# An up projection of seven block-sum products in place of eight block products, in a two-layer hybrid decoder step

## The reference

```python
def conv_ffn(xn, buf, w_up, w_conv, b_conv, w_down):
    u, gt = jnp.split(xn @ w_up, 2, axis=-1)
    t = u.shape[1]
    up = jnp.concatenate([buf.astype(u.dtype), u], axis=1)
    conv = b_conv
    for j in range(CONV_W):
        conv = conv + w_conv[j] * up[:, j:j + t]
    y = (jax.nn.silu(conv) * gt) @ w_down
    return y, up[:, -(CONV_W - 1):]
```

## Time and profile before

| what | value |
|---|---|
| median of three runs | 1718.83 us |
| span of the profiled execution (the page gives no other time for it) | 1719.7 us |
| TensorE matmul / weight load busy | 1637.4 us (95%) / 1481.8 us (86%) |
| VectorE, ScalarE, GpSimd busy | 926.0, 617.1, 181.0 us |
| TensorE instructions | 14807 |
| matmuls of the up projection, L1399 | 4032, 30% of the chain that ended last |
| matmuls of the down projection, L1472 | 2088, 15% of that chain |
| DMA | 219 MB, mean 128 GB/s |

### The profile page before, as it was taken

How to read it: one execution, slowest core, us unless ns; L and a number is a source line. 1 busy time by engine, 2 the same in 40 slices (tenths; PEclk the granted TensorE clock), 3 DMA queues, 4 the chain that set the end, 5 groups by cost and what they waited for, 6 DMA issues and landing times.

```text
span 1719.7 us, 37383 instructions
## 1 busy us (share of the span) xinstructions
PE 1637.4 (95%) x14807; PEld 1481.8 (86%) x14807; DVE 926.0 (54%) x2434; ACT 617.1 (36%) x1215; POOL 181.0 (11%) x290
## 2 busy tenths in 40 slices
PE   6999999988999999999989999998799999999998
PEld 5899875558999999999989997655689999999997
DVE  3544446656564555645564354575656464555644
ACT  3322246534451322413342213664334232423314
POOL 1011104511100000000001101242210000000001
PEclk9999999999999999999989999999999999999999
DMA  9436297468521321221133536634944122322201
GB/s 345 128 97 186 95 362 222 120 207 145 196 88 61 99 99 62 101 84 50 53 100 92 182 114 236 220 89 150 167 114 165 52 98 99 99 79 69 99 25 58
DMA packets 156544, 219.43 MB, mean 128 GB/s; under 512 B 11466, under 2 KB 116362, under 8 KB 155932
## 3 DMA queue, kind: packets, MB, share of 16 engines
q1 hardware_dynamic: 151488, 201.45, 37.5%
q0 software_dynamic: 4896, 15.71, 3.6%
HBM read 208.77 MB, written 16.68 MB: 131 GB/s over the span
## 4 chain that ended last, share of the span: by engine, by line
PE 87%; DVE 4%; DMA 3%; ACT 2%; SPq 1%; issue 1%; DVEq 1%; POOL 1%; ACTq 0%
PE ps L1399 30%; PE ps L1472 15%; PE ps L921 13%; PE ps L1351 5%; PE ps L764 3%; PE ps L1060 2%; PE ps L1045 2%; PE ps L972 2%; DMA slab<-in_w_out 2%; PE ps L905 1%; PE ps L1383 1%; PE ps L916 1%; PE ps L915 1%; PE ps L1017 1%; DMA big<-in_cache_win_kv 1%
## 5 line engine op out<-in xcount | busy, mean ns | idle before, releaser
L1399 PE MATMUL ps<-work_r,big_r 128*128 128x272 f32 x1344 | 279.2, 289 | 2.2 <-ACT work L1910 1.1
L1399 PE MATMUL ps<-work_r,slab_r 128*128 128x272 f32 x1344 | 278.5, 288 | 0.0
L1399 PE MATMUL ps<-xnT_r,big_r 128*128 128x272 f32 x1344 | 276.4, 287 | 0.0
L1399 PEld LDWEIGHTS ps<-work_r,big_r 128*128 128x128 f32 x1344 | 210.1, 188 | 4.7 <-issue 4.7
L1399 PEld LDWEIGHTS ps<-xnT_r,big_r 128*128 128x128 f32 x1344 | 211.7, 188 | 0.0
L1399 PEld LDWEIGHTS ps<-work_r,slab_r 128*128 128x128 f32 x1344 | 210.6, 188 | 0.0
L921 PE MATMUL ps<-slab_r,work_r 128*128 128x256 f32 x960 | 205.6, 282 | 0.0
L2078 DVE TENSOR_TENSOR slab_r<-slab,big_r 128x2048 fp32r<-128x2048 f32 (+1 forms) x84 | 170.7, 2035 | 52.2 <-ACT big_r L1874 42.1
L1913 ACT ACTIVATE big<-big,work 128x560 f32<-128x560 f32 x44 | 33.6, 765 | 371.4 <-DVE big L2736 371.4
L921 PEld LDWEIGHTS ps<-slab_r,work_r 128*128 128x128 f32 x960 | 157.8, 188 | 2.7 <-issue 2.5
L1472 PE MATMUL ps<-side_r,big_r 128*128 128x272 f32 x696 | 145.7, 291 | 0.8 <-DVE big_r L2078 0.8
(11 more groups left out here) (498 smaller groups left out, 3172.2 us busy)
## 6 DMA issues: line engine op xcount, KB each, us to landing
slab<-in_w_mod SPq DMA_DIRECT2D x22, 2048.0 KB, 10.5
slab<-in_w_up SPq DMA_DIRECT2D x44, 1024.0 KB, 7.7
slab<-in_w_in SPq DMA_DIRECT2D x20, 1024.0 KB, 6.4
slab<-in_w_down SPq DMA_DIRECT2D x20, 1024.0 KB, 6.8
slab<-in_cache_cmp_kv SPq DMA_DIRECT2D x128, 128.0 KB, 2.0
slab<-in_cache_sel_kv SPq DMA_DIRECT2D x96, 128.0 KB, 2.1
big<-in_cache_win_kv SPq DMA_DIRECT2D x16, 512.0 KB, 7.5
out<-in_cache_win_kv POOLq DMA_DIRECT2D x16, 508.0 KB
```

What stands on the lines that cost most here:

```text
L1399: ins = mm(ps[2 * half + b][:, 0:HALF], wt, fr(x[:, k, HALF * b:HALF * b + HALF]), start=k == 0 and n == 0, stop=k == KC - 1 and n == 2)
```

## The change

Chunks 0 to 3 stay as they were. For chunks 4 to 21 (CL = 4) the two by two by two block structure of [u; gate] = weights x inputs (weights U_K1, U_K2, G_K1, G_K2 of 512 columns, inputs K1/K2 x t1/t2) is computed with seven products of sums of blocks, M1 to M7, in place of eight products of blocks. Each product is 4 k x 3 = 12 matmuls of 272 columns.

- Per layer, `input_sums` on GpSimd makes four sums of input blocks (T1 to T4, 1088 columns each, eight operations); ScalarE and VectorE split them.
- Per chunk, `block_sum` on GpSimd makes four weight sums of 512 columns. Seven weight operands are split per chunk, in a ring of four slots: the high parts by ScalarE, the low parts of M1, M5, M6, M3, M7 by VectorE, those of M2 and M4 by GpSimd.
- Product results are added in PSUM where two follow each other in one bank (M1 + M6 + M7 + M4 in one, M5 + M3 in another), and ScalarE copies the intermediate sums out (M1, M5, M1 + M6, 272 columns each). VectorE adds the copies back for u's two halves and the gate's second half. The first tap, the tail and the history copies go to ScalarE.
- The loop over chunks is unrolled on all engines. Up weights come one chunk at a time (1 MB, rows of 512 B) into a pair of buffers in slab 2; `split_down` goes in quarters of 1024 columns. Several semaphores are merged.

TensorE's order, and the product:

```diff
-                four_chunks(0, first=True)
-                for j in range(1, NG):
-                    four_chunks(j)
...
+                m1(CL)
+                m2(CL)
+                down(4, 0)
+                m5(CL)
+                m6(CL)
+                m3(CL)
+                m7(CL)
+                for c in range(CL + 1, FC):
+                    m1(c)
+                    m4(c - 1)
+                    m5(c)
+                    m2(c)
+                    m6(c)
+                    if c % 4 == 0:
+                        down(4, c // 4 - 1)
+                    m3(c)
+                    m7(c)
                 down(2, NG, last=True)
...
+                def product(kind, c, bank, new):
+                    n = nth(kind, c)
+                    pe.wait_ge(*low_at(kind, c, L))
+                    xh, xl = FACTOR[kind]
+                    for k in range(4):
+                        wh, wl = [fr(r[n % RING][:, 128 * k:128 * k + 128]) for r in (ring_hi, ring_lo)]
+                        for m, (wt, x) in enumerate(((wh, xh), (wh, xl), (wl, xh))):
+                            ins = mm(ps[bank][:, 0:HALF], wt, fr(x[:, k, :]), start=new and k == 0 and m == 0, stop=k == 3 and m == 2,
+                                     skip_group_check=True)
+                    ins.then_inc(b_acc.sem, 1)
+                def m4(c):
+                    pe.wait_ge(c_g2.sem, c_g2.at(nc_(c), L))
+                    product("M4", c, PBANK[c % 2], False)
```

ScalarE's order:

```diff
+                for c in range(CL + 1, FC):
+                    g, q = c // 4, c % 4
+                    product1_out(c)
+                    high("M6", c)
+                    silu(1, c - 1)
+                    history_in(c)
+                    high("M3", c)
+                    if g < NG and q in (1, 2):
+                        split_down(2 * q - 2, 1)
+                    product5_out(c)
+                    high("M7", c)
+                    split_h((c - 1) % 4, c - 1)
+                    if c + 1 < FC:
+                        high("M1", c + 1)
+                    if g < NG and q in (1, 2):
+                        split_down(2 * q - 1, 1)
+                    sum6_out(c)
+                    high("M4", c)
+                    if c + 1 < FC:
+                        high("M5", c + 1)
...
+                    first_tap(c)
+                    if c + 1 < FC:
+                        high("M2", c + 1)
+                    tail_kept(c)
```

VectorE's order:

```diff
+                for c in range(CL + 1, FC):
+                    g, q = c // 4, c % 4
+                    low_block("M6", c)
+                    hidden_block(c - 1)
+                    low_block("M3", c)
+                    if g < NG and q in (1, 2):
+                        split_down(2 * q - 2, 1, g)
+                    low_block("M7", c)
+                    split_h((c - 1) % 4, c - 1)
+                    u_first(c)
+                    if c + 1 < FC:
+                        low_block("M1", c + 1)
+                    if g < NG and q in (1, 2):
+                        split_down(2 * q - 1, 1, g)
+                    if q == 0:
+                        for m in range(8):
+                            add_y(g - 1, m)
+                    u_second(c)
+                    if c + 1 < FC:
+                        low_block("M5", c + 1)
+                    else:
+                        for part in range(2):
+                            split_down(part, 1, NG)
+                    gate_second(c)
+                    other_taps(c)
```

GpSimd's order, and SP's loads of the up weights:

```diff
+                input_sums()
+                low_block("M2", CL)
...
+                for c in range(CL + 1, FC):
+                    block_sum("M5", c)
+                    low_block("M4", c - 1)
+                    block_sum("M6", c)
+                    low_block("M2", c)
+                    block_sum("M3", c)
+                    block_sum("M7", c)
+                low_block("M4", FC - 1)
...
+                def load_raw(c):
+                    if c < CL + 2:
+                        sp.wait_ge(g_acc.sem, g_acc.at(2, L))
+                        sp.wait_ge(w_hi.sem, w_hi.at(3, L))
+                    else:
+                        sp.wait_ge(*low_at("M4", c - 2, L))
+                    dst = raw_up[c % 2].rearrange("p (h k n) -> p h k n", h=2, k=8)
+                    for h in range(2):
+                        sp.dma_start(dst[:, h, :, :], wup[L, :, :, h, 128 * c:128 * c + 128]).then_inc(raw_loads(c, L)[0], 16)
```

More of the change, by code:

```diff
@@ new lines, in sum_at, with low_at, nc_ @@
+        def sum_at(kind, c, L):
+            return b_sum.sem, b_sum.at(4 + 4 * (c - CL) + ("M5", "M6", "M3", "M7").index(kind) + 1, L)
+        def low_at(kind, c, L):
+            on_pool = kind in LOW_POOL
+            before = [(m, f) for f in range(CL, FC) for m in ROUND if (m in LOW_POOL) == on_pool and nth(m, f) < nth(kind, c)]
+            return b_lo[on_pool].sem, b_lo[on_pool].at(len(before) + 1 + (4 if before and not on_pool else 0), L)
+        def nc_(c):
+            return c - CL + 1
@@ new lines, in _ @@
+                for q in range(CL):
+                    u_chunk(q % 2, q)
+                    if q < 2:
+                        if q == 0:
+                            act.wait_ge(slab_in[0], slab_loads("ffn", 0, L))
+                        split_w(q + 2, q + 2)
+                    if q == 2:
+                        high("M1", CL)
+                    if q == 3:
+                        high("M2", CL)
+                        history_in(CL)
+                    split_h(q, q)
+                    if q == 1:
+                        act.wait_ge(slab_in[1], slab_loads("ffn", 1, L))
+                    for k in ((), (0, 1), (2, 3), ())[q]:
+                        split_down(k, 1)
@@ L2727, in conv @@
                     n = UPW - 2
[L2728 removed]
+                    ts_(cv[:, s, 0:n], up[:, s, 0:n], column(cd), None, ALU.mult)
                     drain()
[L2730 to L2732 removed]
@@ L2768, in _, with add_y @@
[L2768 to L2780 removed]
+                def add_y(g, c):
+                    dve.wait_ge(y_acc.sem, y_acc.at(8 * g + c + 1, L))
+                    b = down_bank(c, g == NG)
+                    residual(c, ps[b], ps[b + 1], 40 + c).then_inc(y_add.sem, 1)
+                    drain()
+                    if g == NG and L + 1 < DEPTH and 2 <= c < 6:
+                        low_first(c - 2, L + 1)
@@ new lines, in _ @@
+                for q in range(CL):
+                    conv(q % 2, q)
+                    hidden(q, q)
+                    if q < 2:
+                        split_w(q + 2, q + 2)
+                    split_h(q, q)
+                    if q == 2:
+                        low_block("M1", CL)
+                    for k in ((), (0, 1), (2, 3), ())[q]:
+                        split_down(k, 1, 0)
+                low_input_sum(0)
+                low_input_sum(1)
+                u_first(CL)
+                for c in range(8):
+                    add_y(0, c)
+                    if c in (0, 1):
+                        low_input_sum(2 + c)
+                    elif c < 6:
+                        low_block(("M5", "M6", "M3", "M7")[c - 2], CL)
@@ L2787, in _ @@
                     norm_scales(96 + 8 * (L + 1), 8)
-                add_y(NG, 0)
+                for m in range(8):
+                    add_y(NG, m)
                 if L + 1 < DEPTH:
```

401 lines of the change are left out of this document (303 added, 98 removed).

## The result

The changed kernel takes 1803.7 us (median of four runs, 1799.5 to 1813.1) against 1719.0 us: a ratio of 1.049, 95% interval 1.046 to 1.053. It is slower, by 85 us where 48 were forecast, and 4 us above the range's upper end. The profiled execution took 1799.5 us with a span of 1797.7.

What follows compares the result with a forecast made beforehand. TensorE's matmuls, 95% of the span, were taken to bound the kernel. From 1718.8 us: -54.5 matmuls + 84 groups + 14 start + 4.8 end = +48, giving 1767 us, range 1680 to 1800.

Steps and rivals of the forecast that it cites:

- Sign and mechanism: Whole kernel: slower by 48 us, because GpSimd operations hold VectorE's SBUF-only instructions; slower given 0.69.
- -54.5 us of matmuls: Feed-forward up projections: 12 matmuls fewer a chunk, 1.515 us each for 36 chunks, if TensorE never waits.
- The hold: Chunk rounds: each GpSimd operation holds VectorE's SBUF-only instructions about 1.1 us; six in every round, 6.6 us.
- the size of the group, +10.5 us: Four chunks between down projections: 52.9 us against 42.4 of TensorE work; four groups in two layers, +84 us.
- The granted clock should stay at its upper level: Profile after the change: TensorE's clock stays at the 2.4 GHz level, as in all slices before.
- The walk: VectorE's work and holds from one down projection's end to the next: 3.7 + 29.0 + 11.9 + 8.3 = 52.9 us.
- 0.9 under the hidden products, since these read PSUM: Rounds with w_down: 0.9 us of the six holds' 6.6 us costs VectorE nothing, falling under hidden's products.
- The start, +7 us a layer: First convolutions behind GpSimd's input sums: stall 5.4 us, 1 to 2 at the next chunk; bounds 0 and 12.
- The end, +2.4: Last chunk of each layer: TensorE idles 3.4 us where it idled 1.0; +4.8 us in all, bounds 0 and +8.
- the first rival: Low parts and taps, rounds 5 to 21: holds cost little, 1.5 us a group, 1 each start; 1683 us, chance 0.28.
- Late raw loads: Rival: up-weight loads with 512 B rows and w_down loads come late; 60 us on top, 1827 us, chance 0.10.
- the likeliest case: Full holds, chance 0.58: own range 1735 to 1797 us, hold work per group 7 to 13, start 0 to 12 a layer.

Runs made afterwards that it cites:

- e1_no_hold: Changed kernel with GpSimd's six operations per chunk cut from 512 to 16 columns (chunk 4's sums full), M2 and M4 using high weights: 1693.0 us, ratio 0.984.
- e8_before_tt: Kernel before plus six independent GpSimd additions of 512 columns, result unused, for each of chunks 4 to 19: 1801.7 us, ratio 1.047.
- e5_hidden_order: Changed kernel with hidden's three multiplications reordered, the two reading PSUM first, the 272-column one with two SBUF inputs last: 1791.9 us, ratio 1.041.
- e7_all_vector: Changed kernel with weight sums, low parts of M2 and M4 and the eight input sums on VectorE, none on GpSimd: 1770.6 us, ratio 1.031.

## Why the prediction was wrong

**Sign and mechanism were right.** -54.5 us of matmuls is what the trace shows (432 fewer), and e1_no_hold without the holds came to 1693, near the 1683 that the prediction gave for its rival without them. The hold, read from three places of the kernel before, is what ate the gain: e8_before_tt reproduces it with no change of the algorithm. By the rule of the Trainium skill's "SBUF — State Buffer", SBUF: two separate sides, VectorE's instructions with two SBUF inputs are shut out by a GpSimd operation that reads SBUF; the two kernels with added work bear out both halves (taps 1.27 to 1.37 with additions, 0.80 with memsets). The advice of the Trainium skill's "GPSIMD Engine Reference", Engine selection, held too: on VectorE the same work was 31 us cheaper.

**The step that failed is the size of the group, +10.5 us.** The four full groups of a layer lost 13.9, 14.5, 14.7 and 13.0: 28 of the 36 us that were missed. For the group at 605.71 the parts are these.

- "The granted clock should stay at its upper level" was false. The down projection took 25.8 us for the 24.0 priced, 1.5 of the 1.8 by a clock of 0.50 at its beginning, behind 2.5 us of idle. It happened in three of the four down projections behind a layer's first, two of them in groups and one in the end.
- The walk from the end of the down projection to the next one gives 52.9 us, and it took 55.1. The two rounds with w_down were 15.1 us each for 14.5, the one without 11.6 for 11.9, and the last stretch, taps to hidden's low part, 9.3 for 8.3, with five GpSimd operations in it where three holds were priced.
- The holds in the rounds were about right in sum: VectorE is busy 52.5 us there and 35.4 in e1_no_hold, 17 more, where the walk has 17.3. What it priced too low is VectorE's own work: 33.2 us by its terms (twice 9.7, 7.4, 5.0, and 1.4 ahead of the first gate half), 35.4 in e1_no_hold, some of it the end of the down projection's additions to the residual. This division is an estimate, since GpSimd's 16-column operations are still there in e1_no_hold.

Single terms were off without deciding. "0.9 under the hidden products, since these read PSUM": only two of three do. The first, 272 columns, has two SBUF inputs in the changed kernel and was held to 1.29 us; I had read its line in the kernel before, not its operands in the change. e5_hidden_order freed it, the hold went to its neighbours, and the rounds gained 0.2 us a group. GpSimd's 512 columns last 1.28 us at the least and 1.51 in the mean with their own waits, not 1.19. The walk also holds a slip: it takes 2.2 us off in the round without w_down where its own three terms add up to 1.8.

**The start, +7 us a layer, was 8.6.** Its mechanism is as forecast, with waits of 5.1 and 0.8 us; the rest is mostly the clock, 0.77 in the 10 us behind the longer one. **The end, +2.4, was 4.6,** and 1.5 of that is the clock in the last full down projection; its chain is as forecast (u's second half, two w_down lows, taps, SiLU, hidden), though the prediction's terms add up to 3.2 us of idle and not 3.4. What the first rival has for a start without holds, 1 us, no run tests: e7_all_vector has no holds, but the sums' work on VectorE, and loses 7.9.

**The rivals.** Late raw loads did not happen: 512 KB landed in 5.0 us in the median between 560 and 760 us, and ScalarE waited 1.1 us in all for w_down. The range failed by 4 us. Its upper end is that of the likeliest case, 13 us a group and 12 a start; groups of 14 us, the clock in them, lie beyond it. The lower end of that case, 1735, is not what its terms give (7 us a group and no loss at the start are 1725).

What stays open: how much of the 111 us between the changed kernel and e1_no_hold is held VectorE time and how much is GpSimd's later results, and what the clock costs inside the rounds, where it was 0.97 and no run changed it alone.

## What to carry to other kernels

Before work is moved to GpSimd, list which VectorE instructions in that stretch have two SBUF inputs (or are fast one-input copies), read from the operands of the changed kernel, and charge each GpSimd operation that reads SBUF as VectorE time too. Here operations of 1.5 us cost VectorE 0.60 us each in e8_before_tt and 0.75 in the changed kernel, and the same operation done by VectorE itself costs it 0.61. So GpSimd's help took no work off VectorE, even though VectorE was the busier engine. Average slack said nothing: what counted is whether the held instructions lie on the chain that the bounding engine waits for. And when an experiment hits its number, look whether the rows moved that were meant to move.

## What was not expected of the hardware

- 192 independent GpSimd additions of 512 columns cost the kernel before 82 us, 0.43 us each, though VectorE was only 54% busy; 17 of the 82 are the clock in the down projections behind the waits.
- A copy of 16 columns can be held as long as a long instruction: mean 0.61 us for 0.17, single ones 1.26.
- A GpSimd memset leaves two-input instructions alone (0.80 us) but lengthens the one-input ones (0.51 to 0.68, 0.17 to 0.25).
- When a held instruction was moved (e5_hidden_order), the hold went to the next ones, and VectorE's total stayed: 1162.0 and 1162.3 us.
- Idle stretches of 2.5 us before a down projection were followed by some 3.3 us at the lower clock; stretches of 1.9 and 1.5 us were not, nor were those filled with 16 matmuls.
